# Eight transposes of a group placed one by one between the matmuls of the next half, instead of as one block before it

## The chip, the cores and the metric

One core of a Trainium2 chip. The metric is the device time of one execution in microseconds (us); before the change the median of three runs is 2802.2 us (2801.0 to 2802.21).

## What is computed

Two layers of an encoder trunk on 256 tokens of width 2048, in float32, cut here to what matters:

```python
for l in range(2):
    h = rms_norm(x)
    z = h @ w_in                       # 2048 x 9216 columns: SGU, q, k, v, memory q, three gates
    y_sgu, y_attn, y_mem = ...         # spatial gating; 8-head attention; 4 heads into 256 memory tokens
    y = sum_i sigmoid(gate_i) * (branch_i @ w_br_i)
    x = x + y @ w_out
    a, b = split(rms_norm(x) @ w_gate_up)
    x = x + (silu(a) * b) @ w_down     # inner width 5632
```

## The kernel before, in words

**Matmuls in three passes.** Every large product is made in float32r with each operand split into a high and a low part: high x high, high x low, low x high. The weights come from memory in one stream, in units of four 128-row tiles by 512 columns. A *half* is half a unit: two row tiles. ScalarE writes its high part `w_hi` (`split`, L585), VectorE subtracts it from the raw weights to get the low part `w_lo` (L846). There are four slots for such halves, so ScalarE may be four halves ahead of TensorE: it waits on `half_used`, which TensorE raises after the last matmul of each half (L346), and TensorE waits on `lo_ready` before each half (L335). For each of the two row tiles and each of the two 128-token blocks a half has three matmuls (L343, L344, L345), so 12 of 512 columns, into one of the accumulators `acc[0..2]`. A *chunk* is the run of halves (mostly eight) that fills an accumulator with 512 output columns. A layer has 488 halves, both layers 976.

**Transposes.** What one stage makes in rows (tokens on the partitions) the next needs with features on the partitions. TensorE turns it: `transposes(src)` (L362) waits until the PSUM tile `tr` is free (`tr_free`), issues eight 128x128 transposes (four for the keys), and raises `tr_done` on the last. ScalarE then copies `tr` out as a high part, either with one instruction (`op_plain`, L607; `turn_out`, L612) or with four with a gain per feature (`op_gain`, L601). VectorE makes the low part from `tr` and the high part (L871, or four of L863) and raises `tr_free`. There is one `tr` tile, so a group of transposes waits for the copies of the one before. A layer has 29 groups (28 of eight, one of four), both layers 58 groups with 456 transposes.

**Who orders the work.** The order of each engine's instructions is written out by hand. TensorE's (L444 to L568) names between which halves a group stands; there is a half on TensorE behind every group before the next group comes. ScalarE's and VectorE's orders have the copy at the place that fits this: after the `split` of the half that TensorE's progress frees at that moment. A `chunk(..., need={h: k})` makes TensorE wait before half `h` until the copies of earlier groups are through (L359).

**Where groups stand close together.** While the memory tokens are projected (L447 to L458) there are groups of `x` after half 6 of the first chunk and after halves 0, 2 and 4 of the second: two halves apart. On ScalarE and VectorE `op_gain` copies stand between them, with sums, a reciprocal root (`rsqrt`, L874, many small instructions) and the splits. After the branches three groups of `y` stand two halves apart (L522 to L526), with `op_plain` copies. In the last part of the down projection (L554 to L559, `LAST` = 3 groups) the copy of a group issued before half 2 is needed at half 4. After the gating unit (L478) VectorE does `op_plain`, then head sums, `rsqrt` and the rotation of the keys (L1089 to L1097), with its splits between. Of the attention heads, `head_turn(0)` (L404) needs `tr` free and the scaled probabilities of head 0 from GpSimd (L292).

**The other queues.** SyncE only loads weights into four raw slots, each after `lo_ready` (L255). GpSimd scales probabilities, loads biases, and loads the memory tokens for the next layer once the last group of `y` is transposed (L318).

Of the kernel before, what the change touches and what calls it, by code (L numbers as in the profile page):

```python
# [30 lines left out]
P = 128  # L31
# [3 lines left out]
TB = SEQ // P  # L35
# [101 lines left out]
def trunk(nc, weights, x_in, mem_in, memT_in, vecs_in, gains_in, sguT_in, rope_in, bias_in, out):  # L137
    with ExitStack() as ctx:
        def sb(name, shape, dt=F32):
            return ctx.enter_context(nc.sbuf_tensor(name, shape, dt))  # L140

        def psum(name, shape):
            return ctx.enter_context(nc.psum_tensor(name, shape, F32))

        def sem(name):
            return ctx.enter_context(nc.semaphore(name))
# [22 lines left out]
        ident = sb("ident", [P, P])  # L169
# [25 lines left out]
        tr = psum("tr", [P, 4, SEQ])  # L195
# [7 lines left out]
        tr_done, tr_free = sem("tr_done"), sem("tr_free")  # L203
# [124 lines left out]
        def _(pe):  # L328
            n = Counts(pe)
            A, B = (a_hi, a_lo), (b_hi, b_lo)  # L330

            def half(acc_i, hi, lo, kt, first, last):


                pe.wait_ge(lo_ready, n.at("half", 2 * RAW_SLOTS + 1))  # L335
                slot = n.n.get("half", 0) % SPLIT_SLOTS
                for k in range(HALF_KT):
                    wh = w_hi[:, slot, k * COLS:(k + 1) * COLS]
                    wl = w_lo[:, slot, k * COLS:(k + 1) * COLS]
                    for t in range(TB):  # L340
                        o = acc[acc_i][:, t, :]
                        tok = slice(t * P, (t + 1) * P)
                        pe.matmul(o, hi[:, kt + k, tok], wh, start=first and k == 0, stop=False)  # L343
                        pe.matmul(o, hi[:, kt + k, tok], wl, start=False, stop=False)  # L344
                        mm = pe.matmul(o, lo[:, kt + k, tok], wh, start=False, stop=last and k == HALF_KT - 1)  # L345
                mm.then_inc(half_used, 1)  # L346
                n.add("half")

            def chunk(acc_i, hi, lo, halves=FULL, kt=0, first=0, upto=None, need=()):


                if first == 0:

                    pe.wait_ge(taken[acc_i], n.at(f"acc{acc_i}", 1))
                    n.add(f"acc{acc_i}")
                for h in range(first, halves if upto is None else upto):
                    if h in need:

                        pe.wait_ge(tr_free, n.at("tr", 1 - need[h]))  # L359
                    half(acc_i, hi, lo, kt + h * HALF_KT, h == 0, h == halves - 1)  # L360

            def transposes(src, blocks=4):  # L362


                pe.wait_ge(tr_free, n.at("tr", 1))
                for b in range(blocks):
                    for t in range(TB):
                        tp = pe.transpose(tr[:, b, t * P:(t + 1) * P], src(b, t), ident[:, :])  # L368
                tp.then_inc(tr_done, 1)
                n.add("tr")  # L370

            def rows_at(r):
# [71 lines left out]
            with n.loop(DEPTH, half=2 * N_UNITS, tr=TR_LAYER, rows=ROWS_LAYER, acc0=ACC_LAYER, acc1=ACC_LAYER,  # L444
                        acc2=NC, head=N_HEADS, turned=N_HEADS, valued=N_HEADS, mem=FULL):

                for h in range(FULL):  # L447
                    n.add("mem")
                    pe.wait_ge(mem_ready, n.at("mem"))
                    chunk(0, *B, first=h, upto=h + 1)  # L450
                    if h == 6:
                        wait_taken(1)
                        transposes(x_at(0))

                for h in range(FULL):
                    chunk(1, *B, first=h, upto=h + 1)
                    if h in (0, 2, 4):
                        transposes(x_at(1 + h // 2))  # L458

                chunk(0, *A, upto=1, need={0: 3})  # L460
                wait_rows()
                transposes(rows_at(R_MK))
                chunk(0, *A, first=1, need={2: 3, 4: 2, 6: 1})

# [861 lines left out]
```

## Time and profile before

| what | value |
| --- | --- |
| time, median of 3 runs | 2802.2 us |
| span of the profiled execution | 2800.6 us |
| TensorE matmul busy | 2772.3 us, 99% |
| TensorE weight load busy | 2297.9 us, 82% |
| VectorE busy | 1576.3 us, 56% |
| ScalarE busy | 1263.5 us, 45% |
| GpSimd busy | 51.5 us, 2% |
| mean granted TensorE clock | 0.997 |
| transposes of L368 | 456 in 58 groups |

The span is that of one profiled execution, from the first to the last instruction; the median is of timed runs and is 1.6 us longer. Matmul records overlap, since a matmul is recorded from its start until its result has left the array, so what one costs is read from the distance between the starts of two in a row and not from its duration.

### The profile page before, as it was taken

Reading aid. Unit: us, or ns where it says so; the run is one execution under the profiler, and the core shown is the slowest. Engines: PE = TensorE matmul, PEld = TensorE weight load, DVE = VectorE, ACT = ScalarE, POOL = GpSimd, SP = SyncE. Lnnn points to the kernel's source line nnn. Section 1 sums busy time; section 2 is a strip of 40 time slices with the busy share of each in tenths; the row PEclk is TensorE's granted clock in tenths of the full one; section 3 lists DMA queues with packets and bytes.
Section 4 is the critical chain, followed back from the end, with each engine's and each line's share of the span. In section 5 each row is a group of like instructions: output and inputs, shape, how many; then the busy total and the mean of one; then the engine's idle time right before and its main releaser. Section 6 shows DMA issues by size and latency. Waiting matters only on the chain.

```text
span 2800.6 us, 34813 instructions
## 1 busy us (share of the span) xinstructions
PE 2772.3 (99%) x12476; PEld 2297.9 (82%) x12476; DVE 1576.3 (56%) x1771; ACT 1263.5 (45%) x1408; POOL 51.5 (2%) x74
## 2 busy tenths in 40 slices
PE   7999999999999999999999999999999999999999
PEld 5888888888888888888878888888888888888887
DVE  6676555565555455555576755555655555554554
ACT  5445444444443344344364455444444443443443
POOL 0001100000000000000000010000000000000000
PEclk9999999999999999999999999999999999999999
DMA  7544455555555555555555544555555555555553
GB/s 289 195 179 156 170 198 204 197 211 189 187 194 189 188 189 187 194 195 184 192 211 191 184 158 177 200 194 199 211 192 182 193 195 183 194 187 190 193 191 139
DMA packets 76457, 535.63 MB, mean 191 GB/s; under 512 B 8720, under 2 KB 8720, under 8 KB 13104
## 3 DMA queue, kind: packets, MB, share of 16 engines
q1 hardware_dynamic: 71776, 515.99, 51.3%
q0 software_dynamic: 4560, 17.96, 2.0%
q8 instruction: 84, 1.38, 0.2%
q14 instruction: 37, 0.30, 0.0%
HBM read 531.81 MB, written 2.10 MB: 191 GB/s over the span
## 4 chain that ended last, share of the span: by engine, by line
PE 96%; DVE 1%; DMA 1%; issue 1%; ACT 1%; DVEq 1%; POOL 0%; SPq 0%; ACTq 0%; POOLq 0%
PE acc L343 31%; PE acc L345 31%; PE acc L344 31%; PE tr L368 2%; DMA raw<-weights 1%; PE tr L432 1%; PE acc L400 1%; PE tr L415 0%; DVE w_lo L846 0%; DMA y<-memT_in 0%; ACT w_hi L585 0%; DVEq L971 0%; ACT b_hi L671 0%; DVEq L901 0%; ACT rows L658 0%
## 5 line engine op out<-in xcount | busy, mean ns | idle before, releaser
L846 DVE TENSOR_TENSOR w_lo<-raw,w_hi 128x1024 fp32r<-128x1024 f32 x976 | 1194.3, 1226 | 1174.4 <-ACT w_hi L585 1169.9
L585 ACT ACTIVATE w_hi<-raw 128x1024 fp32r<-128x1024 f32 x976 | 1034.6, 1061 | 1492.6 <-PE acc L345 1481.9
L343 PE MATMUL acc<-w_hi,a_hi 128*128 128x512 f32 x2560 | 1005.0, 393 | 3.0 <-issue 3.0
L345 PE MATMUL acc<-w_hi,a_lo 128*128 128x512 f32 x2560 | 996.6, 389 | 0.0
L344 PE MATMUL acc<-w_lo,a_hi 128*128 128x512 f32 x2560 | 996.3, 389 | 0.0
L344 PEld LDWEIGHTS acc<-w_lo,a_hi 128*128 128x128 f32 x2560 | 480.8, 188 | 101.9 <-issue 3.4
L345 PEld LDWEIGHTS acc<-w_hi,a_lo 128*128 128x128 f32 x2560 | 480.6, 188 | 100.3
L343 PEld LDWEIGHTS acc<-w_hi,a_hi 128*128 128x128 f32 x2560 | 480.7, 188 | 99.1 <-DVE w_lo L846 0.7
L343 PE MATMUL acc<-w_hi,b_hi 128*128 128x512 f32 x1344 | 527.3, 392 | 14.3 <-DVE b_lo L998 14.3
L344 PE MATMUL acc<-w_lo,b_hi 128*128 128x512 f32 x1344 | 524.6, 390 | 0.0
L345 PE MATMUL acc<-w_hi,b_lo 128*128 128x512 f32 x1344 | 524.4, 390 | 0.0
L343 PEld LDWEIGHTS acc<-w_hi,b_hi 128*128 128x128 f32 x1344 | 253.3, 188 | 67.8 <-issue 16.1
L345 PEld LDWEIGHTS acc<-w_hi,b_lo 128*128 128x128 f32 x1344 | 253.3, 188 | 53.1
L344 PEld LDWEIGHTS acc<-w_lo,b_hi 128*128 128x128 f32 x1344 | 253.3, 188 | 51.6
L1208 DVE SCALAR_TENSOR_TENSOR rows<-acc,stats,rows 128x512 f32<-128x512 f32 x88 | 61.7, 743 | 0.0
L957 DVE TENSOR_TENSOR x<-acc,x 128x1024 f32<-128x1024 f32 x33 | 40.2, 1218 | 9.5 <-PE acc L345 8.6
L871 DVE TENSOR_TENSOR b_lo<-tr,b_hi 128x1024 fp32r<-128x1024 f32 (+1 forms) x32 | 38.9, 1217 | 0.0
L368 PEld LDWEIGHTS tr<-ident,rows 128*128 128x128 f32 x264 | 30.8, 140 | 4.4
L368 PE MATMUL tr<-ident,rows 128*128 128x128 f32 x264 | 34.3, 272 | 0.0
L607 ACT ACTIVATE b_hi<-tr 128x1024 fp32r<-128x1024 f32 (+1 forms) x32 | 32.6, 1019 | 0.0
L863 DVE SCALAR_TENSOR_TENSOR a_lo<-tr,vecs,a_hi 128x256 fp32r<-128x256 f32 x64 | 26.5, 476 | 1.9 <-ACT a_hi L601 1.9
L794 ACT ACTIVATE rows<-acc,stats 128x512 f32<-128x512 f32 x44 | 27.4, 674 | 0.0
(92 smaller groups left out, 659.8 us busy)
## 6 DMA issues: line engine op xcount, KB each, us to landing
raw<-weights SPq DMA_DIRECT2D x488, 1024.0 KB, 4.8
y<-memT_in POOLq DMA_DIRECT2D x12, 512.0 KB, 7.0
bias<-bias_in POOLq DMA_DIRECT2D x24, 256.0 KB, 4.8
rows<-mem_in POOLq DMA_DIRECT2D x2, 2048.0 KB, 13.0
x<-x_in SPq DMA_DIRECT2D x1, 2048.0 KB, 18.8
out<-x SPq DMA_DIRECT2D x4, 512.0 KB, 5.0
qT<-sguT_in POOLq DMA_DIRECT2D x2, 256.0 KB, 13.1
qT<-gains_in POOLq DMA_DIRECT2D x2, 192.0 KB, 14.7
```

The source lines that it names most:

```text
L343: pe.matmul(o, hi[:, kt + k, tok], wh, start=first and k == 0, stop=False)
L344: pe.matmul(o, hi[:, kt + k, tok], wl, start=False, stop=False)
L345: mm = pe.matmul(o, lo[:, kt + k, tok], wh, start=False, stop=last and k == HALF_KT - 1)
L368: tp = pe.transpose(tr[:, b, t * P:(t + 1) * P], src(b, t), ident[:, :])
L400: mm = pe.matmul(scores[:, a % 2, t * SEQ:(t + 1) * SEQ], q_, k_, start=True, stop=True)
L432: mm = pe.matmul(oT_ps[:, a % 2, :], v_, probT(a)[:, k, :], start=k == 0, stop=k == TB - 1)
L585: act.activation(w_hi[:, h % SPLIT_SLOTS, :], raw[:, slot, part * HALF:(part + 1) * HALF], ACT.Copy).then_inc(hi_ready, 1)
L607: act.activation(hi, tr[:, :, :], ACT.Copy).then_inc(op_hi, 1)
L846: dve.tensor_tensor(w_lo[:, h % SPLIT_SLOTS, :], raw[:, slot, part * HALF:(part + 1) * HALF], w_hi[:, h % SPLIT_SLOTS, :].bitcast(F32), AL ...
L871: dve.tensor_tensor(b_lo[:, kt, :], tr[:, :, :], b_hi[:, kt, :].bitcast(F32), ALU.subtract).then_inc(tr_free, 1)
L957: last = dve.tensor_tensor(xc, acc[acc_i][:, :, :], xc, ALU.add)
L1208: last = dve.scalar_tensor_tensor(out=rows[:, r, t, :], in0=acc[acc_i][:, t, :], scalar=rs_ffn[:, t:t + 1], in1=rows[:, R_U, t, :], op0=AL ...
```

## The change

`transposes` no longer issues the transposes. It waits for `tr_free` as before and notes the group as pending. `one_transpose` issues the next transpose of a pending group, and raises `tr_done` with the last. `half` calls it after the first and after the second matmul of each of its four triples, so a half has eight places and a group is over within the half that follows it. Nothing else is changed: the waits ahead of a group, the order on the other engines and the number of instructions are the same.

```diff
+            turning = None
+
+            def one_transpose():
+
+                nonlocal turning
+                if turning is not None:
+                    src, b, t, blocks = turning
+                    tp = pe.transpose(tr[:, b, t * P:(t + 1) * P], src(b, t), ident[:, :])
+                    b, t = (b, t + 1) if t + 1 < TB else (b + 1, 0)
+                    turning = (src, b, t, blocks)
+                    if b == blocks:
+                        tp.then_inc(tr_done, 1)
+                        turning = None
...
                         pe.matmul(o, hi[:, kt + k, tok], wh, start=first and k == 0, stop=False)
+                        one_transpose()
                         pe.matmul(o, hi[:, kt + k, tok], wl, start=False, stop=False)
+                        one_transpose()
                         mm = pe.matmul(o, lo[:, kt + k, tok], wh, start=False, stop=last and k == HALF_KT - 1)
...
             def transposes(src, blocks=4):
 
 
+                nonlocal turning
                 pe.wait_ge(tr_free, n.at("tr", 1))
-                for b in range(blocks):
-                    for t in range(TB):
-                        tp = pe.transpose(tr[:, b, t * P:(t + 1) * P], src(b, t), ident[:, :])
-                tp.then_inc(tr_done, 1)
+                turning = (src, 0, 0, blocks)
                 n.add("tr")
```

## Rows read from the trace of the kernel before

**Rows 1.** The page: span, TensorE's busy time, the chain that ended last.
```profile
span 2800.6 us, 34813 instructions
PE 2772.3 (99%) x12476; PEld 2297.9 (82%) x12476; DVE 1576.3 (56%) x1771; ACT 1263.5 (45%) x1408; POOL 51.5 (2%) x74
PE acc L343 31%; PE acc L345 31%; PE acc L344 31%; PE tr L368 2%; DMA raw<-weights 1%; PE tr L432 1%; PE acc L400 1%; PE tr L415 0%; DVE w_lo L846 0%; DMA y<-memT_in 0%; ACT w_hi L585 0%; DVEq L971 0%; ACT b_hi L671 0%; DVEq L901 0%; ACT rows L658 0%
```

**Rows 2.** Waits of TensorE: waiter, waited for, us in total, times, longest.
```profile
PE acc L343 <- DVE b_lo L998: 14.3, 2, 12.1
PE tr L368 <- DVE a_lo L863: 1.3, 2, 1.1
```

**Rows 3.** Timeline of TensorE around a group: start, us, engine, line, operation, tiles, count.
```profile
2065.33 0.39 PE L343 MATMUL acc<-w_hi,a_hi 128*128 128x512 f32 x1
...
2068.05 0.39 PE L343 MATMUL acc<-w_hi,a_hi 128*128 128x512 f32 x1
...
2070.55 0.39 PE L345 MATMUL acc<-w_hi,a_lo 128*128 128x512 f32 x1
2070.78 1.03 PE L368 MATMUL tr<-ident,x 128*128 128x128 f32 x8
...
2071.88 0.40 PE L344 MATMUL acc<-w_lo,a_hi 128*128 128x512 f32 x1
...
2073.03 0.39 PE L343 MATMUL acc<-w_hi,a_hi 128*128 128x512 f32 x1
```

**Rows 4.** Timeline of weight loads around the same group.
```profile
2070.55 1.02 PEld L368 LDWEIGHTS tr<-ident,x 128*128 128x128 f32 x8
2071.54 0.19 PEld L343 LDWEIGHTS acc<-w_hi,a_hi 128*128 128x128 f32 x1
2071.65 0.19 PEld L344 LDWEIGHTS acc<-w_lo,a_hi 128*128 128x128 f32 x1
2071.89 0.19 PEld L345 LDWEIGHTS acc<-w_hi,a_lo 128*128 128x128 f32 x1
```

**Rows 5.** Timelines: copy with gain after a group (ScalarE, VectorE), 614 to 619.
```profile
615.74 1.55 ACT L601 ACTIVATE a_hi<-tr,vecs 128x256 fp32r<-128x256 f32 x4
617.32 1.66 DVE L863 SCALAR_TENSOR_TENSOR a_lo<-tr,vecs,a_hi 128x256 fp32r<-128x256 f32 x4 [0.24 <-ACT a_hi L601]
```

**Rows 6.** Timelines: plain copy after the last group of transposes, TensorE, ScalarE, VectorE.
```profile
2735.26 1.03 PE L368 MATMUL tr<-ident,rows 128*128 128x128 f32 x8
2736.42 1.01 ACT L607 ACTIVATE b_hi<-tr 128x1024 fp32r<-128x1024 f32 x1
2737.69 1.22 DVE L871 TENSOR_TENSOR b_lo<-tr,b_hi 128x1024 fp32r<-128x1024 f32 x1
```

**Rows 7.** Timelines: copies of each layer's first group; second group of layer 2.
```profile
47.79 1.65 DVE L863 SCALAR_TENSOR_TENSOR a_lo<-tr,vecs,a_hi 128x256 fp32r<-128x256 f32 x4
...
1436.02 1.65 DVE L863 SCALAR_TENSOR_TENSOR a_lo<-tr,vecs,a_hi 128x256 fp32r<-128x256 f32 x4
1437.73 1.09 PE L368 MATMUL tr<-ident,x 128*128 128x128 f32 x8 [0.26 <-DVE a_lo L863]
```

**Rows 8.** Timelines after the gating unit: VectorE's copy, its late splits, TensorE's half.
```profile
144.40 1.22 DVE L871 TENSOR_TENSOR b_lo<-tr,b_hi 128x1024 fp32r<-128x1024 f32 x1
155.78 3.49 DVE L846 TENSOR_TENSOR w_lo<-raw,w_hi 128x1024 fp32r<-128x1024 f32 x3
159.17 0.39 PE L343 MATMUL acc<-w_hi,a_hi 128*128 128x512 f32 x1
```

**Rows 9.** GpSimd scales the probabilities of head 1; TensorE turns them.
```profile
237.32 1.04 POOL L292 TENSOR_TENSOR prob_b<-prob_b,stats 128x512 f32<-128x512 f32 x1 [4.06 <-DVE stats L980]
240.22 0.60 PE L415 MATMUL tr<-ident,prob_b 128*128 128x128 f32 x4
```

**Rows 10.** Stretches: us, busy of each engine (instructions), granted clock, DMA share, GB/s.
```profile
38.00:76.00 38.00, 36.92 (x184) 30.72 (x183) 32.37 (x74) 26.82 (x38) 0.00 (x0) 1.00 0.48 182
1411.00:1414.50 3.50, 3.50 (x10) 2.73 (x9) 1.82 (x3) 0.57 (x2) 0.74 (x2) 0.51 0.93 372
```

## The prediction

> **What bounds the kernel now.** I read the page first: TensorE is busy for 2772.3 of 2800.6 us, and the chain that ended last is 93% the three matmul lines L343 to L345, with the transposes of L368 at 2% [rows 1]. So each slot on TensorE counts, and each wait of TensorE counts; what ScalarE (45%) and VectorE (56%) do is free as long as TensorE doesn't wait for it. Then the waits of TensorE: the large one, 14.3 us, is for the memory tokens at the start of each layer, where no transposes stand; the only one at a group of transposes is 1.3 us, twice, for the copies of the group before [rows 2]. Last the timelines around a group, for what a transpose costs today and what a different neighbour might make of it.
>
> **What a group costs now.** A half without transposes takes 2068.05 - 2065.33 = 2.72 us, 0.2267 a matmul [rows 3]. From the L345 ahead of a group to the fourth matmul after the first triple behind it, seven matmul slots, pass 2073.03 - 2070.55 = 2.48 us; seven slots are 1.59, so the block costs 0.893 us. Its eight transposes: a load starts as the slot of the instruction ahead of its own begins (the first transpose's with the L345 at 2070.55, the transpose itself at 2070.78), so the loads show that the last transpose began at 2071.54 and the L343 behind it at 2071.65 [rows 4]. That is 0.87 us for eight, 0.109 each. The remaining 0.023 us is lost at the two changes of kind: the L343 behind the block has a slot of 0.24 instead of 0.227, its neighbours a few ns. There are 58 groups, 57 counted in eights, so 51 us of transposes in all, the most that is at stake.
>
> **Part 1: the same transposes between matmuls.** Nothing is taken away: as many loads, transposes and matmuls. The block would gain from being broken up only if its slot of 0.109 were set by the load of the next transpose, which a 512-column matmul could cover. But the last transpose of the block is followed by a matmul and its load, as each would be after the change, and its slot is 0.11 too [rows 4]. So I keep 0.109 a transpose. What grows is the number of changes between matmul and transpose: from one pair a group to eight. Below, the cost is nothing, if it is a loss of the group and not of each change; above, each transpose carries the whole 0.023, seven more times, 0.16 us a group and 9.2 us over 57. I take 0.075 a group: the loss lies on the matmul ahead and on some three behind, by 5 to 10 ns each; in the new half each of the 12 matmuls has a transpose on one or both sides, 12 x 0.008 = 0.10, less the 0.023 paid today. 57 x 0.075 = **4.3 us**.
>
> **Part 2: `tr_done` comes later.** Today it comes 0.87 us after the group's start; then with the last place but one matmul of the half. Call H the end of that half. ScalarE's copy starts today 2736.42 - (2735.26 + 0.87) = 0.29 us after the last transpose's slot [rows 6]; that slot will end a matmul (0.23) before H, so the copy starts at H + 0.06. VectorE's starts 2737.69 - 2735.26 = 2.43 us after the group's start today, then 0.89 + 2.72 + 0.08 + 0.06 + 1.27 = 5.02: each copy on VectorE moves by up to 2.6 us against TensorE. Where that meets a wait:
>
> Gain copies two halves apart (third and fourth group of `x`, both layers): from ScalarE's start to VectorE's end 618.98 - 615.74 = 3.24 us [rows 5], so `tr` is free at H + 3.3, and TensorE, with one half in between, is there at H + 2.72. Four waits of 0.6 where there is none today: **2.4 us**. VectorE's head sums and ScalarE's row sums stand before these copies; by their order they are through before H + 1.6, so they add nothing.
>
> The second group of `x`: in layer 1 VectorE's copy at 47.79 stands behind its root and two splits, and ScalarE's part would be there by then, so today's wait stays as it is. In layer 2 TensorE arrives at 1437.31 (idle time counts from the recorded end of the L345, 1437.47, which began 0.39 earlier, plus its slot); H is 2.72 earlier, 1434.6, and VectorE could start at 1434.6 + 0.06 + 1.58 = 1436.3 instead of 1436.02 [rows 7]: **0.3 us**.
>
> Plain copies two halves apart (first and second of `y`, and the last group of the down projection, both layers; six in all): 0.06 + 1.27 + 1.22 = 2.55 after H, before TensorE's 2.72. No wait, with 0.17 us to spare; if the cover is gone each costs what it is short.
>
> After the gating unit VectorE is one chain from its copy at 144.40 to three splits in a row at 155.78. Moved by 2.6, the first ends at 158.38 + 1.23 = 159.6; TensorE wants that half at 159.17, then 159.25 [rows 8]. 0.35 us, twice: **0.7**. Every other split keeps its lead of three halves.
>
> Heads: `turn_out` moves behind half 7, the exponent of head 1 and a split queue behind it on ScalarE, and VectorE's gate and GpSimd's scaling of head 1 behind these, by some 2 us. The scaling ends today at 238.36, TensorE turns that head at 240.22 [rows 9]: about 0.2 us, twice: **0.4**. GpSimd's reload of the memory tokens waits for the last `y` group, 2.6 us later, hundreds of us ahead of its use; SyncE follows VectorE's splits and no slot is short for more than the cases above.
>
> **Sum.** 4.3 + 2.4 + 0.3 + 0.7 + 0.4 = 8.1 us. Against the profiled span 2800.6 that is 2808.7; the median stands 1.6 higher, 2802.2, so I forecast 2810, 0.3% slower. About 0.2%, 5.6 us, is what a measurement of this kernel tells from no change.
>
> **Rivals.**
> *Faster: a transpose is bound by its load.* If the array needs only 128/512 of a matmul's slot, 0.057 us, and the 0.109 is the load of the next transpose, then between matmuls each gives back 0.052: 456 x 0.052 = 23.7, less 3.8 of waits, 2782. It decides if the slot of a transpose with a matmul behind it is below 0.1. Against it stands that very slot in the block, 0.11 [rows 4]; for it only that the first matmul behind a block follows a change of half. Chance 0.07. The Trainium skill (TensorE: Matmul & The Clock Gate, "Wait — 56ns, not 53.3ns?" and "LDWEIGHTS") gives 55.8 ns to a 128-column matmul at full clock and 107 ns to a load; by it the load would set the slot, but the next matmul's load would have to fit under the transpose as well, and the sum would stay as it is.
>
> *No change: the mixing is free.* The 0.023 is a loss of the group, and only the waits remain: 3.8 us, 2806. For it: at the scale of 5 ns nothing in the trace shows a lone transpose between two matmuls. Chance 0.25.
>
> *Slower by much: the clock falls in the mixed halves.* Transposes would be some 24% of such a half (0.87 of 3.6 us). The stretch from 38 to 76 us, the memory projection with its five groups, has the granted clock at 1.00, and the only lower stretch, 0.51, comes behind the long wait at the layer's start [rows 10]. If it fell to 1.2 GHz in the 57 halves, each would cost up to 2.72 us more, 155 us, 2957. Chance 0.01. The Trainium skill (same page, "Part 4: PE-mode transpose") says that transposes do not count as activity for the clock gate; that speaks against spreading them, and the stretch from 38 us does not show it.
>
> *The change doesn't do what it says* can't be: a half stands behind every group and has eight places.
>
> **Chances.** My own case, 0.67, holds 2806 to 2817: mixing between 0.04 and 0.16 a group, waits of 3 to 5.6 us (all six plain copies short by 0.3 add 1.8). Its lower edge is the no-change case. Slower by over 0.2% needs 5.6 us, that is a mixing cost over 0.03 a group: 0.66 of it and the clock case. Within 0.2%: 0.27. Faster: 0.07. The range 2804 to 2817 takes in the bounds of the mixing cost from nothing to full and leaves out the load case, the clock and some of each tail.
>
> **What would show it.** The distance from the start of a matmul to the next one across a transpose: 0.34 to 0.35 us if I am right, 0.29 in the first rival. A half with eight transposes: 3.67 us, against 3.61 with free mixing. In the waits of TensorE: L343 or L345 waiting for VectorE's L863 some six times, 3 to 4 us in all against 1.3; VectorE's L846 once a layer after the gating unit. The granted clock at 1.00 throughout the layers. I am wrong if groups take less than 0.85 us, or if a wait shows at the plain copies of more than 0.3 us, or if any wait grows along a stage instead of standing alone.

## The result, and the profile after

The changed kernel takes 2811.77 us (median of 5 runs, 2811.64 to 2812.02) against 2802.2 of the kernel before: a ratio of 1.0036, 95% interval 1.0024 to 1.0047, so 9.6 us slower where 7.8 were forecast. Runs of one kernel lie in two clusters some 1.5 us apart, so differences of 1 or 2 us are read below from slots and waits, not from medians. The span of the profiled execution is 2810.2 us against 2800.6.

The page after, the lines that answer to [rows 1] (span; busy time of the engines; the chain that ended last):

```profile
span 2810.2 us, 34815 instructions
PE 2779.1 (99%) x12476; PEld 2283.7 (81%) x12476; DVE 1574.7 (56%) x1771; ACT 1262.0 (45%) x1408; POOL 53.3 (2%) x74
PE acc L357 31%; PE acc L359 30%; PE acc L361 30%; PE tr L339 2%; DMA raw<-weights 1%; PE tr L446 1%; PE acc L414 0%; PE tr L429 0%; DMA y<-memT_in 0%; DVE w_lo L860 0%; ACT w_hi L599 0%; ACT a_hi L615 0%; DVE a_lo L877 0%; DVEq L985 0%; DVEq L915 0%
```

L357, L359 and L361 are the three matmul lines (L343 to L345 before), L339 the transpose. The chain is the same chain, 9.6 us longer: nothing has taken TensorE's place as the bound. The waits of TensorE after, against [rows 2]:

```profile
PE acc L357 <- DVE b_lo L1012: 14.2, 2, 12.0
PE acc L357 <- DVE a_lo L877: 3.0, 6, 0.8
PE tr L429 <- POOL prob_b L292: 1.5, 2, 0.8
```

The wait at the layer's start is unchanged. Six waits for VectorE's gain copy (L877) stand where two did, and there is a new one, twice: the transposes of the probabilities of head 1 (L429) wait for GpSimd, while a wait for it of 0.4 us in all at head 0 is gone. Together that is some 3 us more, a third of the loss. The rest doesn't show as waiting here: idle time is counted from the recorded end of the matmul before, so this view leaves out up to 0.17 us of every wait (0.39 less 0.227), and a wait shorter than that wholly. Most of the rest is in the distance of the starts. Two timelines of TensorE, at the first transpose of the last two groups (start, us, count), before (the second is in [rows 6]) and after:

```profile
2690.84 1.03 PE L368 MATMUL tr<-ident,rows 128*128 128x128 f32 x8
```

```profile
2700.52 0.27 PE L339 MATMUL tr<-ident,rows 128*128 128x128 f32 x1
...
2745.04 0.27 PE L339 MATMUL tr<-ident,rows 128*128 128x128 f32 x1
```

From group to group lie 16 halves, 43.52 us of matmuls at 2.72 each. Before, 2735.26 - 2690.84 = 44.42 pass; after, 2745.04 - 2700.52 = 44.52. No engine is late in this stretch, so a group now costs 1.00 us instead of 0.90 (0.893 by the finer reading in the prediction): 0.107 more, and over 57 groups 6.1 us. The other groups agree: where no wait and nothing but matmuls of 512 columns lies between two groups, the same difference has a median of 0.893 before and 1.000 after (42 and 38 distances). The weight loads of such a group tell the slots, because a load starts with the instruction ahead of its own (view: timeline of weight loads, changed kernel):

```profile
2744.82 0.14 PEld L339 LDWEIGHTS tr<-ident,rows 128*128 128x128 f32 x1
2745.05 0.19 PEld L359 LDWEIGHTS acc<-w_lo,b_hi 128*128 128x128 f32 x1
2745.18 0.14 PEld L339 LDWEIGHTS tr<-ident,rows 128*128 128x128 f32 x1
2745.39 0.19 PEld L361 LDWEIGHTS acc<-w_hi,b_lo 128*128 128x128 f32 x1
2745.50 0.19 PEld L357 LDWEIGHTS acc<-w_hi,b_hi 128*128 128x128 f32 x1
```

The second transpose begins at 2745.39 and the matmul behind it at 2745.50: a slot of 0.11, as in the block [rows 4]. The first transpose of the triple can't be read so surely: by the loads it has 0.13 and the matmul behind it 0.21, less than any undisturbed matmul, and only the sum of 0.34 is firm, some 0.007 more than 0.109 + 0.227. Where the matmuls can be read by themselves, they have become dearer: in the half with transposes and in the next one most of their slots are 0.230 to 0.243 instead of 0.227. The tail can be seen from start to start (timeline of TensorE, changed kernel):

```profile
2748.49 0.40 PE L357 MATMUL acc<-w_hi,b_hi 128*128 128x512 f32 x1
...
2749.66 0.39 PE L361 MATMUL acc<-w_hi,b_lo 128*128 128x512 f32 x1
```

Five matmuls pass in 2749.66 - 2748.49 = 1.17 us where 1.13 would be usual, with no transpose between them: the disturbance lives on into the next half.

### The profile page after: what moved, and what is told of

Same layout as the page of the kernel before. It is cut to its first block, busy times and chain, and to the rows that moved or that the text cites. A ratio compares the mean times of both kernels' runs of the same rounds, so it can differ in the third digit from the quotient of the medians.

```text
span 2810.2 us, 34815 instructions
## 1 busy us (share of the span) xinstructions
PE 2779.1 (99%) x12476; PEld 2283.7 (81%) x12476; DVE 1574.7 (56%) x1771; ACT 1262.0 (45%) x1408; POOL 53.3 (2%) x74
## 4 chain that ended last, share of the span: by engine, by line
PE 95%; DVE 1%; DMA 1%; issue 1%; ACT 1%; DVEq 1%; POOL 0%; ACTq 0%; SPq 0%; POOLq 0%
PE acc L357 31%; PE acc L359 30%; PE acc L361 30%; PE tr L339 2%; DMA raw<-weights 1%; PE tr L446 1%; PE acc L414 0%; PE tr L429 0%; DMA y<-memT_in 0%; DVE w_lo L860 0%; ACT w_hi L599 0%; ACT a_hi L615 0%; DVE a_lo L877 0%; DVEq L985 0%; DVEq L915 0%
## 5 line engine op out<-in xcount | busy, mean ns | idle before, releaser
L359 PE MATMUL acc<-w_lo,a_hi 128*128 128x512 f32 x2560 | 1008.0, 394 | 0.0
L357 PE MATMUL acc<-w_hi,a_hi 128*128 128x512 f32 x2560 | 1004.9, 393 | 2.8 <-issue 2.7
L361 PE MATMUL acc<-w_hi,a_lo 128*128 128x512 f32 x2560 | 1007.5, 394 | 0.0
L359 PEld LDWEIGHTS acc<-w_lo,a_hi 128*128 128x128 f32 x2560 | 480.8, 188 | 105.6
L361 PEld LDWEIGHTS acc<-w_hi,a_lo 128*128 128x128 f32 x2560 | 480.9, 188 | 104.4
L357 PEld LDWEIGHTS acc<-w_hi,a_hi 128*128 128x128 f32 x2560 | 481.2, 188 | 100.6 <-issue 3.2
L357 PE MATMUL acc<-w_hi,b_hi 128*128 128x512 f32 x1344 | 526.1, 391 | 17.2 <-DVE b_lo L1012 14.2
L359 PE MATMUL acc<-w_lo,b_hi 128*128 128x512 f32 x1344 | 534.8, 398 | 0.0
L361 PE MATMUL acc<-w_hi,b_lo 128*128 128x512 f32 x1344 | 534.1, 397 | 0.0
L357 PEld LDWEIGHTS acc<-w_hi,b_hi 128*128 128x128 f32 x1344 | 253.4, 189 | 70.2 <-issue 21.7
L359 PEld LDWEIGHTS acc<-w_lo,b_hi 128*128 128x128 f32 x1344 | 252.9, 188 | 58.4
L361 PEld LDWEIGHTS acc<-w_hi,b_lo 128*128 128x128 f32 x1344 | 253.1, 188 | 56.6
L339 PE MATMUL tr<-ident,rows 128*128 128x128 f32 x264 | 71.6, 271 | 0.0
L615 ACT ACTIVATE a_hi<-tr,vecs 128x256 fp32r<-128x256 f32 x64 | 25.1, 475 | 36.9 <-PE tr L339 36.9
L339 PEld LDWEIGHTS tr<-ident,rows 128*128 128x128 f32 x264 | 36.9, 140 | 5.7
L877 DVE SCALAR_TENSOR_TENSOR a_lo<-tr,vecs,a_hi 128x256 fp32r<-128x256 f32 x64 | 26.5, 477 | 26.3 <-ACT a_hi L615 26.2
```

The source lines that it names most:

```text
L877: last = dve.scalar_tensor_tensor(out=lo[:, k, :], in0=tr[:, k - kt0, :], scalar=vecs[:, gain + k:gain + k + 1], in1=hi[:, k, :].bitcast(F ...
```

## The experiments

My theory: two costs of about equal size, the mixing of transposes and matmuls on TensorE, and the later `tr_done`. The rivals: only the delay costs, or only the mixing. Where an edit moves transposes, it is given in words; in the kernels it is a list of how many transposes stand behind each of the twelve matmuls of a half, 1, 1, 0 four times over for the changed kernel. The expectations put a group of the changed kernel at 0.975 or 0.987 us, from shorter readings than the 1.00 above.

### All eight together, but late

```diff
-   one_transpose() behind the first and second matmul of each triple
+   eight times one_transpose() behind the eleventh matmul of the half
```

> All eight transposes stand together again, but at the place of the eighth (ahead of the last matmul of the next half). My theory (two causes of about equal size: 0.0117 us for each further change between matmul and transpose, and waits from tr_done coming later): no mixing, all the waits of the changed kernel: a group costs 0.89 us, 2802.2 + 4.9 = 2807 us. Rival 1 (only the later tr_done costs): 2811.8. Rival 2 (only the mixing costs, the waits would be made up elsewhere): 2802.

2806.76 us (11 runs, 2806.36 to 2808.44) against 2801.2 for the kernel before on the same chip: 1.0019, interval 1.001 to 1.0029. The last two groups of its trace (timeline of TensorE):

```profile
2699.34 0.93 PE L340 MATMUL tr<-ident,rows 128*128 128x128 f32 x7
...
2743.75 1.03 PE L340 MATMUL tr<-ident,rows 128*128 128x128 f32 x8
```

44.41 us: a block costs 0.89 here as it did ahead of the half. Its waits of TensorE:

```profile
PE acc L360 <- DVE a_lo L880: 3.4, 6, 1.0
PE tr L432 <- POOL prob_b L293: 1.3, 2, 0.6
```

They are those of the changed kernel, without its mixing (and a wait of 0.5 us in all for GpSimd at head 0, 0.4 before). So the delay alone costs 5.6 us, and neither rival holds.

### The same mixing, but earlier

```diff
-   one_transpose() behind the first and second matmul of each triple
+   one_transpose() behind each of the first eight matmuls of the half
```

> One transpose behind each of the first eight matmuls of the half: as many changes as in the changed kernel, tr_done some 0.7 us earlier. My theory: a group costs 0.975 us as now (4.7 us in all); the waits of 0.7 us at the third and fourth group of x go, those at the heads shrink: 2807.5 to 2808.5. Rival 1 (only the delay costs): about 2804. Rival 2 (only mixing): 2811.8.

2808.24 us (11 runs, 2806.45 to 2809.03), ratio 1.0023 (1.0014 to 1.0032). A group costs as much as in the changed kernel, and the waits for the third and fourth group of `x` and for GpSimd are gone:

```profile
PE acc L360 <- DVE a_lo L880: 1.4, 2, 1.2
```

```profile
2697.24 0.27 PE L340 MATMUL tr<-ident,rows 128*128 128x128 f32 x1
...
2741.76 0.27 PE L340 MATMUL tr<-ident,rows 128*128 128x128 f32 x1
```

44.52 us. This is the first cost without most of the second, as the late block was the second without the first: by the medians 7.0 us here and 5.6 there. The 1.4 us that stay are the two waits of [rows 2].

### Spread only where groups stand far apart

```diff
-   transposes(x_at(0)); transposes(x_at(1 + h // 2)); transposes(rows_at(R_Q + 1))
+   the same three calls, each group issued at once; all others spread
```

> The four groups of x in the memory projection and the second group of query heads stand as blocks again, the other 48 groups are spread as in the changed kernel. My theory: no wait at VectorE's gain copies and none of the longer ones at the heads, mixing on 47 groups' worth, 3.9 us: 2806. Rival 1 (only delay): 2802.2. Rival 2 (only mixing): 2810.

2807.64 us (11 runs, 2805.49 to 2808.08), ratio 1.0021 (1.0012 to 1.003); span 2804.4. Its waits at transposes are again the two of the kernel before (1.1 us), and GpSimd is waited for only as there, at head 0 (0.3 us). What is left, 6.4 us by the medians and 3.8 by the spans, is the mixing of 48 groups, at 0.107 each 5.0 us; in this profile the second layer also begins at full clock (see the changed kernel's windows below), worth 1.6 us, which brings the spans to 5.4; the other 0.4 is the wait after the gating unit (below), which this edit leaves in. The expectation had 0.082 a group, too little. A rival that knows only the delay would have had 2802.2.

### How the cost of mixing grows

```diff
-   one_transpose() behind the first and second matmul of each triple
+   twice one_transpose() behind the second matmul of each triple
```

> Two transposes together behind the second matmul of each triple: four changes instead of eight, tr_done at the same place. My theory: 0.893 + 3 x 0.0117 = 0.93 us a group, so mixing costs 2.0 instead of 4.7, waits unchanged: 2809. Rival 1 (only delay): 2811.8. Rival 2 (only mixing): 2806. If the loss isn't per change but per transpose that stands away from the block, 2811.8 too, but then with 0.975 us a group.

```diff
-   one_transpose() behind the first and second matmul of each triple
+   four times one_transpose() behind the fifth and the eleventh matmul of the half
```

> Two blocks of four, behind the fifth and the eleventh matmul: two changes of kind instead of eight. The pairs cost about 0.96 us a group over a long stretch (four changes), the singles 0.987 (eight), the one block 0.893. If each change costs 0.023 us until neighbours lie so near that their losses merge, two changes give 0.916 us a group; if any breaking up costs the same fixed sum, 0.96.

Pairs: 2812.01 us (5 runs, 2810.15 to 2812.6), ratio 1.0036 (1.0023 to 1.005). Fours: 2810.77 us in a single run, span 2809.1. The last two groups, pairs first:

```profile
2700.91 0.38 PE L340 MATMUL tr<-ident,rows 128*128 128x128 f32 x2
...
2745.41 0.38 PE L340 MATMUL tr<-ident,rows 128*128 128x128 f32 x2
```

```profile
2700.37 0.60 PE L340 MATMUL tr<-ident,rows 128*128 128x128 f32 x4
...
2744.84 0.60 PE L340 MATMUL tr<-ident,rows 128*128 128x128 f32 x4
```

44.50 and 44.47. Over all the undisturbed distances the medians are 0.893 us a group with one block, 0.958 with two, 0.973 with four, 1.000 with eight singles. Both counts by changes of kind fail, the 0.0117 a change (0.93 for pairs) and the 0.023 a change (0.916 for fours). The other value expected for fours, 0.96 if any breaking up costs the same fixed sum, is met by the fours but not by the rest: breaking the block at all costs 0.065, and going on to pairs and singles 0.015 and 0.027 more. What fits is a loss per disturbed matmul: each piece that is broken off sets off some three to nine matmuls, most of them 3 to 17 ns longer, and where the next comes before they have died down, the losses don't add. The medians don't separate pairs from singles (the gain would be 1.5 us, each spreads over 2); the distance of the groups does.

### Load or stream

```diff
-   tp = pe.transpose(tr[:, b, t * P:(t + 1) * P], src(b, t), ident[:, :])
+   tp = pe.transpose(tr[0:P // 2, b, t * P:(t + 1) * P], src(b, t)[:, 0:P // 2], ident[:, :])
```

Once with the late block, once with the spread places. Half of the transposing is left out; the tile `tr` is filled with zeros once at the start.

> The late block with transposes of the first 64 columns of their source only (the other half of the transposing is left out): the weight load is half as wide, the streamed identity still has 128 columns. If the slot of 0.109 us in a block is set by the streamed columns (my reading), it stays at 0.109 and the group at 0.89 us; if the load sets it (the rival of the prediction), it falls to some 0.055 to 0.06 and the group to about 0.5 us.

> The same half-wide load (the other half of the transposing is left out), with the transposes spread as in the changed kernel. If the extra 0.0117 us of a change comes from the transpose's load being read while the matmul ahead streams, it falls to about half and a group costs some 0.93 us; if it comes from the change itself, from the transpose's stream or from the matmul's own load, the group stays at 0.975 us.

Weight loads of the late block with half the columns:

```profile
2701.79 1.00 PEld L340 LDWEIGHTS tr<-ident,rows 128*64 128x64 f32 x8
2702.78 0.19 PEld L360 LDWEIGHTS acc<-w_hi,a_lo 128*128 128x128 f32 x1
2702.89 0.19 PEld L360 LDWEIGHTS acc<-w_hi,a_hi 128*128 128x128 f32 x1
```

Eight loads start within 2702.78 - 2701.79 = 0.99 us, the first a matmul's slot (0.23) ahead of its transpose, so seven transposes pass in 0.76: 0.109 each with loads half as wide, though the recorded load has shrunk from 0.140 to 0.112 us. So the load doesn't set the slot, and the prediction's fast rival falls. That the stream of 128 columns does was not varied here, but the heads bear it out: their scores, float32 too (L400), stream 256 columns an instruction with loads of 128, and in the kernel before they start 0.215 us apart, twice 0.108. The group did not even stay at 0.89 but rose to 0.95: from group to group 44.46 us,

```profile
2702.02 1.04 PE L340 MATMUL tr<-ident,rows 128*64 128x128 f32 x8
...
2746.48 1.04 PE L340 MATMUL tr<-ident,rows 128*64 128x128 f32 x8
```

with the loss again in the matmuls behind. With spread places a half-wide load gives 44.53, as good as the changed kernel's 44.52. A narrower load thus never lessened the disturbance, and with the block it made it larger; whether the 64 columns or the half of `tr` that is left out does that is open. The times were 2811.03 and 2813.52 us; single runs, and used for their slots only.

### The wait of head 1

```diff
+                    if s % 2 == 0 and 0 <= (s - 8) // 2 < N_HEADS:
+                        head_exp((s - 8) // 2)
                     if s == 10:
                         turn_out(qT[:, 4:8, :])
-                    if s % 2 == 0 and 0 <= (s - 8) // 2 < N_HEADS:
-                        head_exp((s - 8) // 2)
```

> The changed kernel with one thing swapped on ScalarE: the exponent of head 1 comes before the copy of the second group of query heads. My theory for the 0.85 us a layer that TensorE loses at head 1: the exponent waits behind a copy that now comes 2 us later, and behind it VectorE's reciprocal and GpSimd's scaling, which then also runs beside a split of VectorE's and takes 1.94 us instead of 1.04. With the swap the exponent runs in ScalarE's idle time ahead of the copy: the wait at head 1 goes, head 0's stays as short as now, 1.7 us less, 2810. Rival: the delay comes from VectorE's own order (the gate ahead of the reciprocal), then nothing changes, 2811.8; second rival: the copy becomes the late one and head 0 waits for it instead, 2811 to 2812.

The changed kernel shows why it was tried (timelines of ScalarE, VectorE, GpSimd and TensorE; against [rows 9]):

```profile
234.71 1.02 ACT L626 ACTIVATE qT<-tr 128x1024 f32<-128x1024 f32 x1 [2.26 <-PE tr L339]
235.63 0.56 ACT L648 ACTIVATE prob_b<-acc,stats 128x256 f32<-128x256 f32 x1
...
237.81 1.23 DVE L860 TENSOR_TENSOR w_lo<-raw,w_hi 128x1024 fp32r<-128x1024 f32 x1 [2.94 <-ACT w_hi L599]
...
241.41 0.16 DVE L994 RECIPROCAL stats<-stats 128x2 f32<-128x2 f32 x1
...
241.65 1.94 POOL L292 TENSOR_TENSOR prob_b<-prob_b,stats 128x512 f32<-128x512 f32 x1 [5.88 <-DVE stats L994]
...
243.65 0.66 PE L429 MATMUL tr<-ident,prob_b 128*128 128x128 f32 x4 [0.72 <-POOL prob_b L292]
```

ScalarE stands idle for 2.26 us in front of the copy, with the exponent (L648) behind it; the split that follows is late, VectorE's split waits 2.94 us for it, and the gate and the reciprocal (L994) come late with VectorE. With the swap the first exponent runs ahead of the copy (timeline of ScalarE) and TensorE's waits have no line for GpSimd any more:

```profile
233.73 0.56 ACT L648 ACTIVATE prob_b<-acc,stats 128x256 f32<-128x256 f32 x1 [1.18 <-DVE stats L986]
...
234.83 1.02 ACT L626 ACTIVATE qT<-tr 128x1024 f32<-128x1024 f32 x1
```

```profile
PE acc L357 <- DVE b_lo L1012: 14.4, 2, 12.2
PE acc L357 <- DVE a_lo L877: 3.4, 6, 1.2
```

Span 2808.4, 1.8 us below the changed kernel; median 2810.7 (6 runs, 2809.29 to 2811.69), as expected, though 1.1 us between medians alone would prove little. Over the halves around head 1 TensorE loses 0.95 us less than in the changed kernel in the first layer and 0.99 less in the second, so the whole loss at head 1 is given back there. One part of the expectation was wrong: GpSimd's scaling still takes 2.03 us, it only starts 1.0 us earlier, at 240.66.

### The kernel before, with the groups further apart

```diff
-                    if h in (0, 2, 4):
+                    if h in (1, 3, 5):
                         transposes(x_at(1 + h // 2))
```

> Made from the kernel before: blocks as there, but the second to fourth group of x stand behind halves 1, 3 and 5 of their chunk instead of 0, 2 and 4, so that three halves lie between the first and the second. It tests whether the distance of the groups, and not their form, sets the waits for the gain copies: TensorE's waits at a transpose for VectorE's copy (1.3 us in the kernel before) go, and nothing takes their place: 1.6 us under the kernel before, 2800.6 against 2802.2. Rival: ScalarE, one half later with its copy, becomes late with the halves and the time is the same or longer.

2799.69 us (11 runs, 2798.17 to 2800.61) against 2802.0: ratio 0.9992, interval 0.9983 to 1.0001. No wait for VectorE's gain copy is left, and the second group starts at 50.79, nine us after the first, without one:

```profile
41.74 1.03 PE L368 MATMUL tr<-ident,x 128*128 128x128 f32 x8
...
50.79 1.03 PE L368 MATMUL tr<-ident,x 128*128 128x128 f32 x8
```

The span is 2.2 us shorter than that of the kernel before, 1.9 of it by the starts of the halves in the two memory projections (1.35 and 0.53). It is the fastest kernel here, as forecast and for the reason forecast, but the interval reaches 1, so the run alone doesn't prove it faster.

## Why the prediction was right, point by point

**The bound.** Right: TensorE's slots and waits are all that moved.

**The slot of a transpose.** Right as far as it can be read: 0.109 in the block, early or late, and with loads half as wide; 0.11 for the second transpose of a triple, with the sum across the first one at 0.34, the forecast's own sign. A half with eight transposes takes 3.68 us, forecast at 3.67 and at 3.61 with free mixing.

**The price of mixing.** Right in kind, short in size. The text took "0.075 a group", 4.3 us; it measured 0.107, 6.1 us. The step that fell short is "in the new half each of the 12 matmuls has a transpose on one or both sides, 12 x 0.008": the count stopped at the end of the half, and some eight matmuls of the next one are longer as well. The picture under it, a loss on matmuls near a transpose, holds, without a reason for it; its upper bound, every transpose with the full 0.023, was not reached, because near losses don't add.

**The gain copies two halves apart.** Four waits of 0.6 and 0.3 us in the second layer were forecast, 2.7 us. Over the halves between the first and the last group of these stages, less 0.107 a group, TensorE lost 1.1 us in the first layer and 1.6 in the second: 2.7, as forecast. One of them (timelines of ScalarE, VectorE and TensorE: the third group of the first layer waits for the copy of the second):

```profile
53.34 1.57 ACT L615 ACTIVATE a_hi<-tr,vecs 128x256 fp32r<-128x256 f32 x4 [2.19 <-PE tr L339]
54.94 1.66 DVE L877 SCALAR_TENSOR_TENSOR a_lo<-tr,vecs,a_hi 128x256 fp32r<-128x256 f32 x4 [1.63 <-ACT a_hi L615]
56.73 0.50 PE L357 MATMUL acc<-w_hi,b_hi 128*128 128x512 f32 x1 [0.45 <-DVE a_lo L877]
```

ScalarE and VectorE had been idle for 2.19 and 1.63 us and did the copy as soon as it could be done; TensorE then waited 0.45 us by its idle time, which counts from the recorded end of the matmul before, and 0.6 by its slot.

**Plain copies.** No wait for them shows, as forecast with 0.17 us to spare.

**After the gating unit.** "159.6; TensorE wants that half at 159.17" named the right half and the right cause, and was too much in size: 0.35 us a layer forecast, 0.23 measured, 0.5 us for both. The half that began at 159.17 before has its low part from the first split of the row, and begins at 161.25 (VectorE and TensorE, changed kernel):

```profile
159.98 4.62 DVE L860 TENSOR_TENSOR w_lo<-raw,w_hi 128x1024 fp32r<-128x1024 f32 x4
...
160.96 0.39 PE L361 MATMUL acc<-w_hi,a_lo 128*128 128x512 f32 x1
161.25 0.50 PE L357 MATMUL acc<-w_hi,a_hi 128*128 128x512 f32 x1
161.59 0.40 PE L359 MATMUL acc<-w_lo,a_hi 128*128 128x512 f32 x1
```

A split takes 1.23, so this one is over at 161.20, and TensorE starts 0.05 later, 0.06 later than its slots alone would have it; the first matmul then has a slot of 0.34 and the next ten are mostly some ns longer, 0.17 in all with the first. No idle time is recorded for it. With the early places the same split is over 0.68 us ahead of its half, and that half loses nothing:

```profile
157.69 4.63 DVE L863 TENSOR_TENSOR w_lo<-raw,w_hi 128x1024 fp32r<-128x1024 f32 x4
...
159.58 0.39 PE L360 MATMUL acc<-w_hi,a_hi 128*128 128x512 f32 x1
```

VectorE's chain moved by 2.2 us against TensorE (159.98 - 155.78, less 161.19 - 159.17), not by 2.6. Part of the difference is the lag of 1.27 us from ScalarE's copy to VectorE's, which was read where VectorE was busy with a split [rows 6]. Here it was idle, and the lag is 1.06:

```profile
147.52 1.02 ACT L621 ACTIVATE b_hi<-tr 128x1024 fp32r<-128x1024 f32 x1 [2.39 <-PE tr L339]
148.58 1.22 DVE L885 TENSOR_TENSOR b_lo<-tr,b_hi 128x1024 fp32r<-128x1024 f32 x1 [2.19 <-ACT b_hi L621]
```

**Heads.** "About 0.2 us, twice" was 0.9, twice, 1.8 us. The mechanism was the one named, and the swap shows it; the size was off because the scaling was priced at the 1.04 us of [rows 9]. It took 1.94 us. The trace of the kernel before already had both prices: the scaling for head 0 takes 1.98 us there.

**What no step held.** In the profiled execution before, TensorE's clock was granted at 0.51 in a stretch of 3.5 us at the second layer's start [rows 10]. That is almost all of it at the lower of the two levels, 1.2 GHz. After, TensorE waits as long there, but the stretches at and behind the wait are at 1.00, the upper one, 2.4 GHz:

```profile
1413.50:1417.00 3.50, 1.31 (x7) 1.05 (x6) 2.31 (x5) 3.31 (x7) 2.38 (x5) 1.00 0.81 255
1416.00:1430.00 14.00, 14.00 (x63) 11.56 (x63) 11.37 (x18) 9.76 (x18) 1.18 (x3) 1.00 0.94 356
```

By the starts of the halves there, that gave back 1.6 us in this pair of profiles. It doesn't come from the spreading alone: the early places, the pairs and the fours have the fall, and of the runs of the kernel before some have a mean granted clock of 1.000, which leaves no room for it. So the terms are 6.1 + 2.7 + 1.8 + 0.5, 11.1 where the sum had 8.1, less 1.6 for the clock: 9.5 of the 9.6 us between the spans. The forecast was right by its reasons, but part of its nearness is luck: the mixing and the heads were priced too low, 3 us together with the smaller errors, and in this pair of profiles the clock gave 1.6 back. What the clock is worth in the medians the runs don't show; with 3 us more the time would still have been in the range. (The chances by size, 0.67, 0.27 and 0.07, add up to 1.01.)

**The clock rival.** Nothing of it is seen: the granted clock stands at 1.00 through the mixed halves of both layers. The rule of the Trainium skill (TensorE: Matmul & The Clock Gate, "Part 4: PE-mode transpose"), that transposes don't count as activity in the same way, has no consequence in this trace.

## What to carry to other kernels

Where an engine is busy throughout, ask of a reordering what it gives back: a transpose whose slot isn't set by its load gains nothing from a neighbour that could hide that load, and the loads around a block show this before anything is built. Count separately what the new place does to the signal behind the last instruction: every copy that waits for it moves, and where the next group is near, TensorE pays. Narrowing one operand of the suspected instruction, or keeping the block and moving only its place, tells two such causes apart in one run each.

## What I had not expected

The cost of breaking up a block of transposes: 0.89 us for one block of eight, 0.96 for two pieces, 0.97 for four, 1.00 for eight singles; wherever matmuls and transposes can be told apart, it lies on the 512-column matmuls near them, up to nine behind the last. Even a block of half-wide loads, unbroken, costs 0.95 us, with each transpose at 0.109. Nor does it take a transpose: behind the short wait at 161.25, with no group near, the slots run 0.239, 0.236, 0.232, 0.237, 0.224, 0.231, 0.236, 0.228, much as behind the last transpose of a spread group (0.235, 0.234, 0.225, 0.231, 0.236, 0.228). That looks like the trace of any break in an even run of matmuls; why a matmul is longer then stays open.

GpSimd's scaling of 128x512 takes 1.04 us or about 2 us. In the changed kernel it took 1.94, starting at 241.65 beside this split (timeline of VectorE):

```profile
241.49 1.21 DVE L860 TENSOR_TENSOR w_lo<-raw,w_hi 128x1024 fp32r<-128x1024 f32 x1
```

In the kernel before it took 1.04 for the same head, from 237.32 on, and the split that began beside it at 237.94 took longer than usual:

```profile
237.94 1.51 DVE L846 TENSOR_TENSOR w_lo<-raw,w_hi 128x1024 fp32r<-128x1024 f32 x1 [0.69 <-ACT w_hi L585]
```

All scalings of the two kernels' traces fit: of 24 in each, the slow ones are the two of head 0 before (1.98 us) and the four of heads 0 and 1 after (1.94 to 1.98), and they are the only ones that begin some 0.15 us behind a split; all others take 1.03 to 1.05. It looks as if whoever starts second on the two engines is the one that is held up; this was not tried by itself. The Trainium skill (Advanced Engine Details and Errata, "Mode Summary") says that VectorE's second port is shared with GpSimd and that the two block each other in its two-port modes; the direction agrees, whether these splits run in such a mode no run here shows.
